# Out projection in split products, plain unit order and a new end in a hybrid mLSTM, attention and mixture-of-experts kernel

## What is computed

```python
hm = mlstm_chunkwise(mq, mk, mv, mi, mf)                 # 4 heads of 128
hm = hm * lax.rsqrt(jnp.mean(hm * hm, axis=-1, keepdims=True) + RMS_EPS)
hm = (hm.reshape(b_, s, M_WIDTH) * mlstm_norm[l]).astype(x.dtype)
hm = jax.nn.sigmoid(mo) * hm
ha = swa_sink_attention(aq, ak, av, bias_band, sinks[l])  # 8 heads of 64
x = x + jnp.concatenate([hm, ha], axis=-1) @ w_out[l]
x = x + hier_moe(rmsnorm(x, norm_ffn[l]), ...)           # 16 experts, top-2 in the best of 4 groups
return rmsnorm(x, norm_final)
# in hier_moe, for each expert e:
y = (jax.nn.silu(xt @ w_gate[e]) * (xt @ w_up[e])) @ w_down[e]
out = out + combine[:, e:e + 1] * y
```

## Time and profile before

| what | value |
|---|---|
| median of 3 runs | 1065.23 us (1063.89 to 1067.74) |
| profiled execution, its own time | 1067.88 us |
| its span, first to last instruction | 1066.0 us |
| PE busy | 970.0 us, 91% |
| DVE, ACT, POOL busy | 639.9, 452.4, 253.1 us |
| mean granted clock of TensorE | 0.96 |

### The profile page before, as it was taken

One profiled execution on the slowest core, in us unless ns is written; L12 is line 12 of the kernel. 1 busy time (PEld: TensorE's weight loads), 2 busy tenths in 40 slices (PEclk: granted clock), 3 DMA queues, 4 the chain that ended last, 5 costly groups with the idle time before them and its releaser, 6 DMA issues.

```text
span 1066.0 us, 14902 instructions
## 1 busy us (share of the span) xinstructions
PE 970.0 (91%) x5095; PEld 781.3 (73%) x5096; DVE 639.9 (60%) x1010; ACT 452.4 (42%) x673; POOL 253.1 (24%) x306
## 2 busy tenths in 40 slices
PE   4899999999998899999749999999999999999981
PEld 3598777789997677776637788777777777787861
DVE  5523177774336656665767865666758577665554
ACT  5321344442224132222315745656556475654450
POOL 2200000000000001000026524545435364532233
PEclk9899999999999999999659999999999999999996
DMA  7332111112034521216538977797979888887383
GB/s 266 88 86 63 39 40 40 41 50 80 31 110 144 202 99 60 79 60 237 178 121 311 321 237 236 235 314 211 301 244 299 286 262 261 272 288 216 103 267 147
DMA packets 86256, 184.55 MB, mean 173 GB/s; under 512 B 8339, under 2 KB 29024, under 8 KB 86210
## 3 DMA queue, kind: packets, MB, share of 16 engines
q1 hardware_dynamic: 76114, 153.55, 41.7%
q0 software_dynamic: 9952, 29.86, 11.0%
q10 hardware_dynamic: 144, 0.52, 0.2%
HBM read 151.93 MB, written 31.42 MB: 172 GB/s over the span
## 4 chain that ended last, share of the span: by engine, by line
PE 70%; DVE 14%; issue 7%; ACT 5%; POOL 2%; DMA 0%; DVEq 0%; ACTq 0%; POOLq 0%
PE PS L1671 18%; PE PS L1673 17%; PE PS L1672 17%; PE PS L1831 4%; PE PS L1943 2%; DVE WL L1456 2%; ACT WH L1014 2%; PE PS L1919 1%; DVE HL L1573 1%; DVE WP L558 1%; DVE HB L1581 1%; PE PS L1846 1%; PE PS L1902 1%; DVE XL L1568 1%; PE PS L1803 1%
## 5 line engine op out<-in xcount | busy, mean ns | idle before, releaser
L1456 DVE TENSOR_TENSOR WL<-RAW,WH 128x2048 fp32r<-128x2048 f32 x94 | 213.9, 2289 | 103.8 <-ACT WH L1014 102.6
L1014 ACT ACTIVATE WH<-RAW 128x2048 fp32r<-128x2048 f32 x96 | 184.1, 1918 | 12.4 <-PE PS L1673 10.9
L1671 PE MATMUL PS<-WH,XH 128*128 128x512 f32 x400 | 166.3, 416 | 13.3 <-issue 7.1
L1673 PE MATMUL PS<-WH,XL 128*128 128x512 f32 x400 | 158.4, 396 | 0.0
L1672 PE MATMUL PS<-WL,XH 128*128 128x512 f32 x400 | 157.8, 395 | 0.0
L1671 PEld LDWEIGHTS PS<-WH,XH 128*128 128x128 f32 x400 | 76.2, 191 | 34.8 <-issue 21.6
L765 POOL TENSOR_TENSOR dst<-dst,stat 128x4 f32<-128x4 f32 x8 | 8.1, 1014 | 351.6 <-DVE dst L1408 351.6
L1671 PE MATMUL PS<-WH,HH 128*128 128x512 f32 x200 | 79.8, 399 | 10.9 <-DVE HL L1573 10.9
L776 POOL TENSOR_TENSOR stat<-stat 128x1 f32<-128x1 f32 x93 | 58.6, 634 | 127.4 <-ACT YB L1068 107.5
L1673 PEld LDWEIGHTS PS<-WH,XL 128*128 128x128 f32 x400 | 76.2, 191 | 17.2
L1672 PEld LDWEIGHTS PS<-WL,XH 128*128 128x128 f32 x400 | 76.5, 191 | 13.5
(11 more groups left out here) (351 smaller groups left out, 1849.9 us busy)
## 6 DMA issues: line engine op xcount, KB each, us to landing
RAW<-in_w_gate_dram SPq DMA_DIRECT2D x32, 1024.0 KB, 8.5
RAW<-in_w_up_dram SPq DMA_DIRECT2D x32, 1024.0 KB, 11.6
RAW<-in_w_down_dram SPq DMA_DIRECT2D x32, 1024.0 KB, 5.0
wraw<-in_w_in_dram SPq DMA_DIRECT2D x22, 512.0 KB, 4.6
XT<-in_x_dram SPq DMA_DIRECT2D x8, 512.0 KB, 9.4
vo_dram<-vo SPq DMA_DIRECT2D x16, 256.0 KB, 2.1
wout<-in_w_out_dram SPq DMA_DIRECT2D x4, 1024.0 KB, 7.8
VM<-vo_dram SPq DMA_DIRECT2D x16, 256.0 KB, 6.1
```

The source lines that it names most:

```text
L1014: A(WH[:, d % SPLITS, :], RAW[:, j, :], ACT.Copy).then_inc(s_whi, 1)
L1456: V.tensor_tensor(WLS[d % SPLITS][:, :], RAW[:, TURN[d][1] if d else 0, :], WH[:, d % SPLITS, :].bitcast(fp32), ALU.subtract).then_inc(s_w ...
L1671: mm(bank, ah, bh, start=start, stop=False)
L1673: return mm(bank, al, bh, start=False, stop=stop)
```

## The change

Four parts:

1. The mLSTM half of the out projection becomes 12 split matmuls per (tile, half). ScalarE writes HTH (128 rows, one buffer) in place of hT, VectorE makes HTL in each step; WMH and WML are the halves of the out weights, made in step 0 by four ScalarE copies and four VectorE differences. xr gets one buffer in place of two, and its load on SP waits for the sum of the tile before.
2. `tab2` and all that makes it is removed; the units run in the order of `tab`: S S S S D D D D D S D D S D S D. A unit beyond the last (`idle_`) gets a column of its own in `tab`.
3. At the start of unit 0 the low halves of row groups 2 and 3 come behind the third weight piece, and TensorE's wait for them moves.
4. At the end the last weight piece's high half goes behind the first two squares, a low half goes ahead of HB's second pass, the last rows come before tile 6, and SP instead of GpSimd waits for the last scatter.

```diff
@@ buffers @@
-        hT = at("hT", hn_at, [P, H, S])
+        HTH = at("HTH", hn_at, [P, H, P], f32r)
+        HTL = at("HTL", hn_at + 2 * KB, [P, H, P], f32r)
-        xr = at("xr", pre_at, [P, 2, D])
+        xr = at("xr", pre_at, [P, D])
@@ SP @@
-                sp.dma_start(xr[:, c % 2, :], x2d[c * P:(c + 1) * P, :]).then_inc((s_xr0, s_xr1)[c % 2], 16)
+                if c >= 1:
+                    sp.wait_ge(s_x2, 2 * c)
+                sp.dma_start(xr[:, :], x2d[c * P:(c + 1) * P, :]).then_inc((s_xr0, s_xr1)[c % 2], 16)
...
-            sp.wait_ge(s_tab, 2)
             sp.dma_start(comb_dram.rearrange("(t p e) o -> p t (e o)", p=P, e=NE), comb[:, :, :]).then_inc(s_cmbst, 16)
...
+            sp.wait_ge(s_sca, 32 * n_loop + 96)
+            nc.sync.sem_inc(s_f4, 1)
@@ POOL @@
-            pool.wait_ge(s_sca, 32 * n_loop + 96)
-            settle(50)
@@ ACT @@
+                    if s >= 2:
+                        act.wait_ge(s_wo, 2 * s - 2)
+                    A(HTH[:, :, :], PS[:, 3, :].rearrange("p (a b) -> p a b", a=4), ACT.Copy).then_inc(s_hte, 1)
...
+                if s == 0:
+                    act.wait_ge(s_wout, 32)
+                    for i in range(4):
+                        act.wait_ge(s_vst[i], 64)
+                    for k in range(4):
+                        A(WMH[k][:, :], wout[:, k, :], ACT.Copy).then_inc(s_wmh, 1)
@@ DVE @@
+                if 1 <= s <= NT:
+                    dve.wait_ge(s_hte, s)
+                    V.tensor_tensor(HTL[:, :, :], PS[:, 3, :].rearrange("p (a b) -> p a b", a=4),
+                                    HTH[:, :, :].bitcast(fp32), ALU.subtract).then_inc(s_htl, 1)
...
+                if s == 0:
+                    for k in range(4):
+                        dve.wait_ge(s_wmh, k + 1)
+                        V.tensor_tensor(WML[:, k, :], wout[:, k, :], WMH[k][:, :].bitcast(fp32), ALU.subtract)
@@ PE @@
-                    last = mm(PS[:, 5 + half, :], hT[:, k, P * c:P * c + P], wout[:, k, cols_],
-                              start=False, stop=(k == 3))
+                    last = split3(PS[:, 5 + half, :], HTH[:, k, :], HTL[:, k, :],
+                                  WMH[k][:, cols_], WML[:, k, cols_], False, k == 3)
...
-            pe.wait_ge(s_tab, 2)
```

More of the change, by code:

```diff
@@ L203, in build @@
         vo = at("vo", pre_at, [P, 4, 2, 256])
-        xr = at("xr", pre_at, [P, 2, D])
+        xr = at("xr", pre_at, [P, D])
+        WMH = [at(f"WMH{k}", hn_at + 4 * KB * (k + 1) if k < 3 else pre_at + 4 * KB, [P, D], f32r) for k in range(4)]
+        WML = at("WML", ring_at, [P, 4, D], f32r)
         biasb_at = region(4 * 1160)
@@ L419, in build @@
         s_hte = semaphore("s_hte")
+        HTL_BASE = 2 * H
+        s_htl = s_silu
         s_woh = semaphore("s_woh")
@@ L808, in _ @@
             pool.wait_ge(s_tab, 1)
-            gather(1, 1, 1, tab)
+            gather(1, 1, 1)
             gather_half(1, idxcs[1], 1)
             pool.wait_ge(s_ids, 1)
-            pool.wait_ge(s_tab, 2)
             pool.wait_ge(s_cmbst, 16)
@@ L823, in unit @@
                     gather(u + 2, 3 * u + 2, par)
-                    second = pool.value_load(tab2[0:1, bass.ds(u + 2 + NU, 1)], min_val=0, max_val=1)
+                    second = pool.value_load(tab[0:1, bass.ds(u + 2 + NU, 1)], min_val=0, max_val=1)
                     with pool.If(second > 0):
@@ L1306, in x2_half @@
                 V.tensor_tensor(VM[:, c, 512 * half:512 * half + 512], PS[:, 5 + half, :],
-                                xr[:, c % 2, 512 * half:512 * half + 512], ALU.add).then_inc(s_x2, 1)
+                                xr[:, 512 * half:512 * half + 512], ALU.add).then_inc(s_x2, 1)
             def top2(c):
@@ L1493, in _ @@
[L1493 to L1510, removed]
@@ L1533, in ordered_table @@
[L1533 to L1537, removed]
-                V.tensor_scalar(tab2[:, 2 * NU:3 * NU], PS[:, 5, 2 * NU:3 * NU], 2.0, None,
-                                ALU.mult).then_inc(s_tab, 1)
-            order_values()
+            link(V.tensor_tensor(kk_[:, :], kk_[:, :], idle_[:, :], ALU.add))
+            V.tensor_scalar(tab[:, 2 * NU:3 * NU], kk_[:, :], 2.0, float(COLS), ALU.mult, ALU.min).then_inc(s_tab, 1)
@@ L1610, in _ @@
             lo_piece(0, 2)
+            x_lo(0, 2, 0)
+            x_lo(0, 3, 0)
             lo_piece(0, 3)
@@ L1622, in _ @@
                                        ALU.add, ALU.mult).then_inc(s_sil, 1)
+            last_lo_piece(u, 5)
             dve.wait_ge(s_sil, 2 * u + 2)
@@ L1628, in _ @@
                                        ALU.mult, ALU.mult).then_inc(s_hb, 1)
-            last_lo_piece(u, 5)
             hidden_lo(u, 0, 1)
@@ L1640, in scale, with last_rows @@
                 V.scalar_tensor_tensor(tile, tile, rstd_of(c), nfin, ALU.mult, ALU.mult).then_inc(s_f4, 1)
-            dve.wait_ge(s_nfin, 16)
-            variance(0)
-            for c in range(NT):
-                if c + 1 < NT:
-                    variance(c + 1)
-                scale(c, tile_of(c))
-            dve.wait_ge(s_gath[0], 16 * n_loop + 64)
-            for n, hf in enumerate((1, 0)):
+            def last_rows(n, hf):
                 if hf:
@@ L1658, in _ @@
                 V.scalar_tensor_tensor(row, y, 0.5, row, ALU.mult, ALU.add).then_inc(s_fz, 1)
+            dve.wait_ge(s_nfin, 16)
+            variance(0)
+            for c in range(NT):
+                if c == 6:
+                    dve.wait_ge(s_gath[0], 16 * n_loop + 64)
+                    last_rows(0, 1)
+                    last_rows(1, 0)
+                if c + 1 < NT:
+                    variance(c + 1)
+                scale(c, tile_of(c))
             for n, hf in enumerate((1, 0)):
@@ L1933, in _ @@
             mm(PS[:, 2, 8:8 + 3 * NU + 1], ones[0:NE, :], acu[:, :], start=True, stop=True).then_inc(s_cnt, 1)
-            for i in range(3):
-                mm(PS[0:NU, 4, i:i + 1], acu[:, NU * i:NU * i + NU], ones[0:NE, 0:1], start=True, stop=True)
-            mm(PS[0:NU, 4, 3:4], ones[0:NE, 0:NU], acu[:, 3 * NU:], start=True, stop=True).then_inc(s_cnt, 1)
-            pe.wait_ge(s_uni, 3)
-            mm(PS[0:NU, 4, 4:5], C("tri", NU)[:, 0:NU], uv[:, 1:2], start=True, stop=True).then_inc(s_cnt, 1)
             def x_group(g, par):
@@ L2026, in unit @@
                 down(5, 0, 0, 1).then_inc(s_wused, 1)
-            pe.wait_ge(s_uni, 4)
-            mm(PS[0:NU, 4, 8:8 + NU], ones[0:NU, 0:NU], uw[:, :], start=True, stop=True).then_inc(s_cnt, 1)
             pe.wait_ge(s_gath[0], 32)
@@ L2036, in _ @@
             pe.wait_ge(s_wlo, 1)
-            with pe.If(has_second(0, tab) > 0):
+            with pe.If(has_second(0) > 0):
                 gate_up(0, 0, 0, 1)
             gate_up(0, 0, 0, 0).then_inc(s_wused, 1)
-            pe.wait_ge(s_uni, 5)
-            mm(PS[:, 5, 0:3 * NU], ones[0:NU, :], ur[:, :, :].rearrange("p a b -> p (a b)"),
-               start=True, stop=True).then_inc(s_cnt, 1)
             x_group(2, 0)
             x_group(3, 0)
-            pe.wait_ge(s_tab, 2)
             with pe.Fori(0, MAXU - 1, 2) as u:
```

62 lines of the change are left out of this document (16 added, 46 removed).

## The result

| | before | changed |
|---|---|---|
| median, 5 runs each | 1065.64 us | 1056.63 us (1055.98 to 1058.77) |
| ratio, 95% interval | | 0.9916 (0.9897 to 0.9934) |
| profiled execution | 1067.88 us | 1055.98 us |

The changed kernel is faster by 9.0 us by the medians (7.0 to 11.0 by the interval). The prediction was 1056.8.

What follows compares the result with a forecast made beforehand. TensorE, busy 970 of 1066 us, was taken as the bound, so its waits count. Terms +7.4, -3.9, +1.1, -9.0, +0.6, -2.2 and -2.4 sum to -8.4: 1059.5 us, or 1056.8 as median; range 1050 to 1066.

Steps and rivals of the forecast that it cites:

- halves of the weights: Step 0 into 1: four VectorE differences ahead of kw make it late and TensorE waits; +7.4 us.
- products: mLSTM out projection: twelve split matmuls save 0.65 us a group, counted for six groups only; -3.9 us.
- single xr, late store: Last tiles: the xr load waits, tile 5's xn store lands late and delays the square reusing its buffer; +1.1 us.
- start of the units: Gate 0 to the unit loop: without the sorted table TensorE waits only for the gather and starts sooner; -9.0 us.
- order: Units: four one-half units in front and five two-half units behind change TensorE's waits between units; +0.6 us.
- hidden rows, exit: Kernel end: last hidden rows ready earlier, -2.2 us; GpSimd leaves without waiting for the last scatter, -2.4 us.
- Rivals 1 and 2: Units 0 to 3: a run of one-half units starves on DMA; priced at 1062, chance 0.14, or slower than before, 0.12.
- Rival 4: mLSTM steps: VectorE's and ScalarE's chain binds, so the split gains nothing, plus longer cold stretch; 1061 to 1066, chance 0.08.
- Rival 5: mLSTM steps: slack behind half 0 lets the products save 10.4 us instead of 3.9; 1050, chance 0.04.
- Rival 3: Unit start and kernel end: waiting for comb takes 5 of the 9 us, the exit's 2.4 don't come; 1063, chance 0.12.

Runs made afterwards that it cites:

- lows_later: Changed kernel with the four out-weight differences cut into column halves and put behind kw, ptm and qs of step 1; 0.9854 against the kernel before.
- order_only: Kernel before with only the sorted table removed, plain unit order and the new start of the units; 0.9920, -8.5 us.
- end_only: Kernel before with only the new end: earlier hidden rows and the last scatter's wait off GpSimd; 0.9957, -4.6 us.
- plain_keys: Kernel before, sort and its waits kept, but keyed by unit number so that only the order of units changes; 1.0001.
- no_split: Changed kernel with plain fp32 products and two xr buffers again; 0.9862 against the kernel before, -14.7 us.
- split_only: Kernel before with only the split products of the mLSTM rows and the single xr buffer; 1.0029, +3.1 us.
- xnb_first_before: Kernel before with VectorE making xnb ahead of the next step's exponents instead of behind them; 0.9989, -1.2 us.
- xnb_first: Changed kernel with later weight differences and earlier store of tile 5's xn, plus xnb made ahead of the exponents; 0.9839 against before, its base 0.9824.
- exit_on_pool: Changed kernel with later weight differences and earlier xn store, the last scatter's wait and settle back on GpSimd; 0.9846 against before, its base 0.9824.
- xn_early: Changed kernel with SP's store of tile 5's xn ahead of its xr load for tile 7 and the weight pieces; 0.9871 against before, -13.7 us.

## Why the prediction was right, step by step

| step | predicted | between the traces | on the chip alone |
|---|---|---|---|
| halves of the weights | +7.4 | +7.1 | |
| products | -3.9 | -5.4 | |
| single xr, late store | +1.1 | +2.4 | |
| the three together | +4.6 | +4.1 | +3.1 (1.6 to 4.6) |
| start of the units | -9.0 | -11.3 | |
| order | +0.6 | +0.3 | 0.0 (-1.6 to 1.9) |
| both | -8.4 | -11.0 | -8.5 (-11.0 to -6.1) |
| hidden rows, exit | -2.2, -2.4 | -2.3, -2.6 | -4.6 (-6.3 to -2.8) |
| sum | -8.4 | -11.8 | -9.0 (-11.0 to -7.0) |

*Weight halves.* Place, cause and size as forecast: 363.54 for a predicted 363.9, and lows_later gives 6.6 us back.

*Products.* Each of six steps gave 0.67 for a forecast 0.65, and half 0's saving became a longer wait for xnb, 5.6 us in place of 1.3. The other 1.1 us, in step 5, is clock. There the trace of before has a stretch at the lower clock that the trace after lacks, with TensorE busy throughout:

```profile
417.00:421.00 4.00, 4.00 (x30) 3.62 (x30) 1.91 (x9) 1.53 (x3) 0.75 (x2) 1.00 0.71 262
421.00:425.00 4.00, 4.00 (x11) 2.98 (x10) 2.62 (x11) 0.00 (x0) 1.01 (x1) 0.57 0.00 0
```

The traces of order_only, end_only, plain_keys and no_split, which have the plain products too, show it within 3 us of that place; that of split_only doesn't. xnb_first_before has one at 462 to 466 us. With split products there are such stretches too, in xnb_first and, from 496 to 501 us, in lows_later and exit_on_pool, so whether the split moves them or the execution does is open. I had not seen it ahead.

*Single xr.* Mechanism right, size too small, by more than half: the term was +1.1 and measured 2.4. I had counted 10.3 us to landing from the store's own issue. In both traces it landed some 16 us behind the first weight piece (484.19 to 500.1 before, 502.24 to 518.8 after), whenever it was issued itself, so the store made the square 2.4 late and not 1.6. And the discount from 1.6 to 1.1, for other work of TensorE in between, did not come: TensorE's offset goes from 1.0 at the group ahead (516.12 against 515.09) to 3.4 at the transposes of xnb (521.83 against 518.43). xn_early gives the 2.4 back and more.

*Start.* Gate 0 bound by the gather: right. Its gain was forecast as 2.4; behind the gather the trace gives 2.6. The 1.1 ahead of the gather was not in the sum. Clock may be part of it: from 516 to 520 us before ran at 0.58 of full speed and the changed kernel at 0.98, but the start as before can have either, since plain_keys had 0.72 there and end_only 1.00. From gate 0 to product j=1 the forecast was 5.0 and the trace gives 5.3; behind that 1.6 for the clock, and the trace gives 2.2. On the chip order and start together are 8.5, near the forecast. The two profiled executions differ by more. They ran at different mean clocks, 0.960 and 0.968. 17 runs of before on one chip go from 1063.9 us at 0.968 to 1070.2 at 0.951 (those at 0.960 lie from 1065.2 to 1068.1), and a run of the changed kernel at 0.956 took 1058.8 where those at 0.968 took 1056.0 to 1057.2. By an estimate from these, some 2 to 3 of the 11.9 us are the clock of the execution that happened to be profiled.

*Order, end, exit.* As forecast. Rivals 1 and 2, the starved run of S units, did not occur: from 568 to 640 us the queues carry 321 GB/s at a share of 0.96 in the changed kernel, S units take 23.0 us, and TensorE's waits over all units don't grow; plain_keys, with the same run of S units alone, costs nothing that shows. Rival 4 has a true half: the split part alone is a loss, +3.1, though the products do gain; its place is kw and the store. Its longer stretch at the lower clock is there (to 369 us, in place of 363 before), but costs little: the offset is 7.06 at kw and 6.79 in step 2. Rival 5, the whole gain, did not occur: one group a step shows. Rival 3 fell with order_only, where the start keeps 8.5, and with exit_on_pool.

The forecast of the whole was right also because its errors were small and of both signs; each of the three parts alone was within its interval, the split with its 4.6 at the very edge. That it came within 0.2 us is luck: the traces have the single xr 1.3 us dearer and the products and the start together 3.8 better than forecast, and part of that is clock that no term held.

## What to carry to other kernels

A one-time preparation on an engine that runs in order costs what stands behind it, not what it takes: the same differences (4.6 us in four pieces, 5.0 in eight) cost 7 us ahead of kw and 0.6 at most behind qs. When a load gets a new wait, look for what is queued behind it on its queue: here a small store went behind 4 MB of weights, and moving one line brought 4.8 us (3.3 of it seen in the trace). Products that become shorter pay only up to the next wait, and a whole that is faster can hold a part that is slower, so run each part alone.

## What was not expected of the hardware

TensorE's granted clock fell to the lower of its two levels for three to four us in stretches in which the engine had no gap: 421 to 425 us in before, 418 to 422 and 438 to 443 in xnb_first. The spread of before's runs, 6 us, goes loosely with their mean granted clock, but not in every kernel: the five runs of lows_later have 1050.7 to 1051.7 us at 0.958 and 1053.5 at 0.963. The Trainium skill (TensorE: Matmul & The Clock Gate, HAM oscillation) ties the lower level to idle gaps; that is what 357 to 369 us of the changed kernel look like (0.60, TensorE busy for 4.57 of 12 us), but not these stretches. What brings them on stays open. GpSimd's exit took 8.2 us both in exit_on_pool, behind the landed scatter, and in its base, where it began at 1039.2 while the scatter was still under way (landing takes 3.4 us from its start in exit_on_pool, which would be 1041.6 here).
